# Order of the first tile's products, place of the positions' fetch, and the engine that sums the squares of a two-block transformer kernel's first stage

## The reference

```python
xf = x.astype(jnp.float32)
y = xf * lax.rsqrt(jnp.mean(xf * xf, axis=-1, keepdims=True) + NORM_EPS)
h = (y * g.astype(jnp.float32)).astype(x.dtype)
proj = h @ w_in                      # 2048 x 7240, split into queries, keys, values, gates
...
ang = positions.astype(jnp.float32)[..., None] * inv_freq
cos, sin = jnp.cos(ang), jnp.sin(ang)
```

## Time and profile before

| | |
|---|---|
| time, median of 3 runs | 1852.86 us (1852.66 to 1852.92) |
| the profiled execution's own time | 1853.12 us |
| its span, first to last instruction | 1851.4 us |
| PE busy | 1823.4 us, 98% of the span |
| DVE, ACT, POOL busy | 57%, 36%, 2% |
| first product of the first stage starts | 8.31 us |
| sum of squares (end of the first stage) | 52.24 us |

### The profile page before, as it was taken

The page is one execution under the profiler, slowest core; times in us unless marked ns, Lnnn a source line. Parts: engine busy times, 40 slices in busy tenths (PEclk is TensorE's granted clock), DMA queues, the critical chain, the costliest instruction groups (busy, mean ns, idle before and its releaser), DMA issues.

```text
span 1851.4 us, 25537 instructions
## 1 busy us (share of the span) xinstructions
PE 1823.4 (98%) x9060; PEld 1514.8 (82%) x9060; DVE 1047.4 (57%) x1768; ACT 665.6 (36%) x1279; POOL 36.3 (2%) x58
## 2 busy tenths in 40 slices
PE   9999999999999999999999999999999999999997
PEld 7788888888888887878868887888888888888887
DVE  7643434444433787853348954766767566665334
ACT  6532332322223544432226342433433333443222
POOL 0000000000000000000002000000000000000001
PEclk9999999999999999999999999999999999999998
DMA  6322222222232333232237363211112222124333
GB/s 237 106 86 91 79 79 91 86 84 82 89 102 80 126 114 113 91 112 93 91 101 218 102 227 124 70 57 57 68 57 69 92 68 79 66 70 136 115 115 102
DMA packets 56021, 186.16 MB, mean 101 GB/s; under 512 B 6688, under 2 KB 11168, under 8 KB 55456
## 3 DMA queue, kind: packets, MB, share of 16 engines
q1 hardware_dynamic: 51328, 170.78, 27.6%
q0 software_dynamic: 4640, 14.68, 3.0%
HBM read 177.05 MB, written 8.39 MB: 100 GB/s over the span
## 4 chain that ended last, share of the span: by engine, by line
PE 90%; DVE 5%; DVEq 2%; ACT 1%; issue 1%; POOL 0%; POOLq 0%; ACTq 0%
PE strip L421 23%; PE strip L423 22%; PE strip L422 22%; PE scores L421 4%; PE scores L422 3%; PE scores L423 3%; PE outputs L423 2%; PE outputs L422 2%; PE outputs L421 1%; PE scores L476 1%; PE scores L869 1%; PE scores L828 1%; PE scores L897 1%; DVE wl L1433 1%; DVEq L1438 0%
## 5 line engine op out<-in xcount | busy, mean ns | idle before, releaser
L421 PE MATMUL strip<-xh,wh 128*128 128x512 f32 (+1 forms) x1976 | 779.7, 395 | 5.7 <-DVE xl L1825 3.2
L423 PE MATMUL strip<-xh,wl 128*128 128x512 f32 (+1 forms) x1976 | 768.0, 389 | 0.0
L422 PE MATMUL strip<-xl,wh 128*128 128x512 f32 (+1 forms) x1976 | 767.2, 388 | 0.0
L421 PEld LDWEIGHTS strip<-xh,wh 128*128 128x128 f32 x1976 | 371.9, 188 | 82.4 <-DVE xl L1825 4.8
L423 PEld LDWEIGHTS strip<-xh,wl 128*128 128x128 f32 x1976 | 371.6, 188 | 77.3
L422 PEld LDWEIGHTS strip<-xl,wh 128*128 128x128 f32 x1976 | 372.3, 188 | 72.7 <-issue 0.7
L1433 DVE TENSOR_TENSOR wl<-raw,wh 128x1024 fp32r<-128x1024 f32 (+3 forms) x306 | 354.7, 1177 | 119.1 <-ACT wh L979 118.2
L979 ACT ACTIVATE wh<-raw 128x1024 fp32r<-128x1024 f32 (+3 forms) x308 | 306.9, 1023 | 109.7 <-PE strip L423 107.1
L1001 ACT ACTIVATE prob<-scores,nms 128x128 f32<-128x128 f32 (+3 forms) x128 | 65.9, 532 | 129.7 <-DVE nms L1481 129.7
L1241 ACT ACTIVATE e_t<-o 128x512 f32 (+1 forms) x30 | 19.0, 632 | 222.0 <-DVE o L1902 118.1
L421 PE MATMUL scores<-xh,wh 128*128 128x512 f32 (+1 forms) x240 | 91.6, 382 | 0.0
(11 more groups left out here) (426 smaller groups left out, 1875.6 us busy)
## 6 DMA issues: line engine op xcount, KB each, us to landing
raw<-in_w SPq DMA_DIRECT2D x308, 512.0 KB, 3.2
xn<-o POOLq DMA_DIRECT2D x4, 1024.0 KB, 7.8
xr<-xn POOLq DMA_DIRECT2D x16, 256.0 KB, 3.0
o<-in_xt SPq DMA_DIRECT2D x7, 512.0 KB, 7.9
o<-in_xt POOLq DMA_DIRECT2D x14, 256.0 KB, 6.3
out<-o SPq DMA_DIRECT2D x14, 256.0 KB, 2.7
raw<-in_w SPq DMA_DIRECT2D x2, 256.0 KB, 4.6
o<-in_xt SPq DMA_DIRECT2D x2, 256.0 KB, 5.1
```

The source lines that it names most:

```text
L421: pe.matmul(out, ah, bh, start=first, stop=False, skip_group_check=shared)
L422: pe.matmul(out, ah, bl, start=False, stop=False, skip_group_check=shared)
L423: return pe.matmul(out, al, bh, start=False, stop=last, skip_group_check=shared)
```

## The change

- Four warming products in place of five.
- The 12 products of the first x tile go pass by pass: the four strips with high by high, as soon as `xh` and the first `wh` are there, then the four with the low weights, then the four with `xl`.
- POOL clears `acc` and adds all 16 squares into it (it was DVE); `pe_sum` waits for the sixteenth of these additions.
- POOL waits for the second tile of x (`x_in[1]`) before it fetches the positions.

```diff
-WARM_FIRST, WARM_MID = 5, 6
+WARM_FIRST, WARM_MID = 4, 6
...
         g.memset(nrt[:, :], 0.0).then_inc(warm, 1)
+        g.memset(acc[:, :], 0.0)
+        g.wait_ge(x_in[1], 16)
         g.dma_start(posi[:, :], d["pos"]).then_inc(pos_in, 16)
+        for j in range(KT):
+            g.drain()
+            g.wait_ge(sq_done, j + 1)
+            g.tensor_tensor(acc[:, :], acc[:, :], sq[j % 2][:, :], ALU.add).then_inc(sq_used, 1)
...
+            if halved and u == 0:
+                pe.wait_ge(first_hi, 1)
+                pe.wait_ge(x_hi, 1)
+                for s in range(4):
+                    pe.matmul(outs[s][:, :], wh[0][:, P * s:P * s + P], xh[:, 0, :], start=True, stop=False)
+                pe.wait_ge(first_lo, 1)
+                for s in range(4):
+                    pe.matmul(outs[s][:, :], wl[0][:, P * s:P * s + P], xh[:, 0, :], start=False, stop=False)
+                pe.wait_ge(x_lo, 1)
+                for s in range(4):
+                    pe.matmul(outs[s][:, :], wh[0][:, P * s:P * s + P], xl[:, 0, :], start=False, stop=False)
+                steps = steps[4:]
...
     def pe_sum(pe, i, squares=acc):
 
-        pe.wait_ge(acc_ready, i + 1)
+        if i == 0:
+            pe.wait_ge(sq_used, KT)
+        else:
+            pe.wait_ge(acc_ready, i)
...
-        v_.memset(acc[:, :], 0.0)
         v_.wait_ge(first_hi, 1)
...
-            else:
-                square_in(j - 1, 0)
...
-        square_in(KT - 1, 0)
-        v_.drain().then_inc(acc_ready, 1)
```

More of the change, by code:

```diff
@@ L527, in pe_four @@
                     pe.wait_ge(x_lo, count + j + 1)
-                    if halved and j == 0:
-                        pe.wait_ge(first_lo, 1)
-                    else:
-                        pe.wait_ge(w_lo, u0 + u + 1)
+                    pe.wait_ge(w_lo, u0 + u + 1)
                 slot = (u0 + u) % SLOTS
@@ L944, in half_sums @@
         def half_sums(hf):
-            pe.wait_ge(acc_ready, 6 + hf)
+            pe.wait_ge(acc_ready, 5 + hf)
             for t in (2 * hf, 2 * hf + 1):
```

## The result

The changed kernel takes 1863.63 us (median of 4 runs, 1862.31 to 1865.08), the kernel before 1852.89 us on the same chip: ratio 1.0058, with a 95% interval of 1.004 to 1.0075. So it is slower by 10.7 us, twice the forecast +5 and 1.6 us above the range. The profiled run took 1862.31 us and is the lowest of the four; its span of 1860.6 us is 9.2 us above the span of before.

The account below looks back on a forecast made before the run. PE, busy 98% of the span, was taken as the bound. The start's -0.85 us and DVE blocked by POOL gave +6.0 (early) or +2.7 to +4.4 (late); +5.0 was taken: 1853.1 + 5.0 = 1858.1 us, range 1851.8 to 1862.

Parts of the forecast that it names:

- Direction and mechanism: First stage: slower, as POOL additions and DVE instructions with two SBUF inputs block each other in full turns; 48%, +3.7 to +8.
- Rival 1: First stage: POOL and DVE hardly block each other, so only the start's -0.85 us remains, 1852.2 us; chance 27%.
- Size of an addition: First stage: one 128x512 addition on POOL takes 1.22 us, bounded by 0.69 and 1.38.
- What DVE loses: First stage: some 15 POOL additions each hold up one DVE instruction by 1.1 to 1.22 us, 16.5 to 18.3 in all.
- The late account: End of the first stage: last `xl` ready at 50.1 to 51.9 us, sum of squares later by 2.7 to 4.4.
- The early account: Sixth `xl`: eleven DVE instructions held up 12.1 us, ready at 28.3, PE stalls 6.8; less 0.85, +6.0 us.
- I take +5.0: Whole change: 5.0 us slower, 1858.1 us, below the +6.0 of the larger account because that needs perfect turns.
- So I give that a small part: PE's clock behind a stall of several us: a lower level, worth 2.9 us at warming, might cost; given a small part.
- The start: First product: starts at 7.45 to 7.53 us instead of 8.31, without waiting for `xl`; gain taken as -0.85 us.
- Behind the stage everything is as before ... move with the sum: After the first stage: the chain to `rb` and PE's 1.06 us wait behind it only shift with the sum.
- Positions at no cost: Later fetch of the positions: there by 18 us at the worst, before DVE's angles; cost zero, at worst 0.5 us.

Follow-up runs that it names:

- own_adds: The kernel before plus sixteen same-size additions on POOL, on its own buffers, whose result nobody uses or waits for; 1868.03 us, ratio 1.0082.
- own_clears: The kernel before plus sixteen POOL clears of a 128x1024 buffer, which only write; 1856.9 us, ratio 1.0016.
- squares_only: The kernel before with only the squares' additions moved to POOL, positions still fetched at the start; 1862.49 us, ratio 1.0048.
- tail_only: The kernel before with DVE's `nrm` ahead of `cum` and `sin_t`, and ACT's `wh` of units 8 and 9 ahead of the sines; 1852.92 us, ratio 0.9994.
- start_only: The changed kernel with the sixteen additions of squares back on DVE; 1854.45 us, ratio 1.0001.

## Why the prediction was right and wrong

- **Direction and mechanism: right.** Reading additions on POOL block DVE's two-input instructions. own_adds shows it without any dependency, own_clears that writes don't. Rival 1, which had 27%, is out: with no blocking `xl` would have kept its 0.75 us.
- **Size of an addition: right.** Estimated 1.22 us, measured 1.27.
- **What DVE loses: a little too high.** The late account had 16.5 to 18.3 us; after has 12.8, squares_only 15.5 (`xl` 6.7, `wl` 4.1, angles 4.7 in single-input instructions). About 0.8 to 1.0 us for each addition.
- **The early account: right for squares_only, by luck for after.** It had the sixth `xl` ready at 28.3, with eleven DVE instructions held up by 12.1 us. In squares_only eleven are held up by 10.4 us and it is ready at 27.6. In after it is ready at 28.6, but only six are held up, by 5.9 us; DVE idles for 7.2 us in the same time, 4.2 of it for the wait of POOL behind the drain, which I hadn't foreseen. The account had a stall of 6.8; there were two of 1.9 and 3.9 in after, and of 0.7 and 4.4 in squares_only. The late account, with waits only near 50 us, did not decide.
- **"I take +5.0": wrong.** I went below the early account because it needs perfect turns. The larger account decided, as the sentence ahead of it says it must; it was the number to take.
- **"So I give that a small part": the step that failed.** The clock behind a stall was priced from both sides (up to 2.9 us) and then left out of the forecast, because the one gap of before, 1.06 us, showed nothing. In after the lower level cost 3.3 us in the stage; the early account with it, +6.0 + 3.3, less the extra 1.0 of the start, is +8.3, and the sum moved by 8.05. That it comes so near is in part the luck of the point above.
- **The start: 1.9 us in place of 0.85 at the first product.** Two things came on top. The first two tiles of x landed in 3.9 us (median), not 5.1, and the first `xh` started at 5.43 instead of 6.75; I had allowed 0.6 us for that. Waiting for the second tile is not needed for it: in the five runs that issue the positions at 1.80 to 2.26 us, behind one or two clears more than before, `xh` starts at 5.11 to 5.86, while tail_only, which issues them at 1.44 like before, has 6.63. And the warming reached the upper level near 5.2 us instead of 7.2, by which PE was free at 6.39. That moment differs from run to run (near 5.5 in tail_only, whose start is that of before), and no run shows that the change set it.
- **"Behind the stage everything is as before ... move with the sum": wrong in both directions.** For an earlier sum it doesn't hold, since DVE's `nrm` had 0.26 us of room (start_only). For the later sum of after, PE's wait for `yv` grew by 0.4 us, with 0.50 us of issue in front of `rb`, and a further 0.7 us of the span lies behind that. This 1.1 us is the difference between 8.05 and 9.2; of the 1.5 us from there to the 10.7 of the medians, 1.3 is that the profiled run was the lowest of the four and 0.2 that the profiled run of before was above its median.
- **Positions at no cost: right for DVE, wrong for POOL.** They landed at 13.6, ahead of the angles at 21.1, but the drain made POOL wait for them.

## What to carry to other kernels

Before work is moved from DVE to GpSimd, count the two-input DVE instructions that run beside it: here each 128x512 addition that reads SBUF on GpSimd took 0.8 to 1.0 us from DVE, no less than the 0.79 us that it relieved it of, so the move could not pay. Price a stall of the matmul engine of about 2 us and more with the clock that may fall behind it (1.5 to 2.4 us here), and take the account that the argument names as deciding. When products start earlier, look for the first instruction on the path behind them that stands in another engine's queue: a gain stops there.

## What the runs showed that was not expected

- The medians of before differed by 1.2 us between the sessions (1852.89 to 1854.04), and the runs of start_only by 5 us (1850.6 at a mean granted clock of 0.996, 1855.6 at 0.992). For a change of about 1 us, eleven runs were not enough.
